# Four adaLN weight units of layer 0 move from the input projection to the output projection

## The reference, cut to what matters

```python
mod_lat = jnp.split(silu(c) @ ada_w[layer] + ada_b[layer], 6, axis=-1)
h = modulate(x, pre_mix_g, mod[0], mod[1])      # norm0: shift, scale
y = concat([a, b]) @ w_out                      # two attentions, one out projection
x = x + mod[2] * rms_norm(y, post_mix_g)        # norm1: gate
h = modulate(x, pre_ffn_g, mod[3], mod[4])      # norm1: shift, scale
x = x + mod[5] * rms_norm(conv_ffn(h), post_ffn_g)   # norm2: gate
```

## Time and profile before

| | kernel before |
|---|---|
| median of three timed executions | 1761.1 us (1760.04 to 1762.46) |
| profiled execution, span from first to last instruction | 1759.0 us |
| TensorE busy | 1687.6 us, 96% of the span |
| VectorE busy | 1026.4 us |
| ScalarE busy | 643.8 us |
| GpSimd busy | 277.3 us |
| mean granted TensorE clock | 0.991 |
| DMA | 224.27 MB, mean 127 GB/s |

### The profile page before, as it was taken

One profiled execution on the slowest core, in us unless ns is written; L12 is line 12 of the kernel. 1 busy time (PEld: TensorE's weight loads), 2 busy tenths in 40 slices (PEclk: granted clock), 3 DMA queues, 4 the chain that ended last, 5 costly groups with the idle time before them and its releaser, 6 DMA issues.

```text
span 1759.0 us, 26977 instructions
## 1 busy us (share of the span) xinstructions
PE 1687.6 (96%) x10042; PEld 1353.9 (77%) x10042; DVE 1026.4 (58%) x1938; ACT 643.8 (37%) x1090; POOL 277.3 (16%) x394
## 2 busy tenths in 40 slices
PE   5998899999999999999999999998999999999998
PEld 2876566668898888888888878875678788888886
DVE  4656565764747777777785681166743744443445
ACT  3323555663321212222324343245643333332343
POOL 1414333330300000000000031046421300000000
PEclk9999999999999999999999999999999999999999
DMA  8589441275513343434343543372503433332243
GB/s 314 191 262 304 108 111 24 46 95 190 190 52 97 103 136 106 132 113 127 97 144 108 179 168 126 114 186 58 145 10 108 144 96 95 95 95 81 86 133 132
DMA packets 265528, 224.27 MB, mean 127 GB/s; under 512 B 75224, under 2 KB 226136, under 8 KB 265432
## 3 DMA queue, kind: packets, MB, share of 16 engines
q1 hardware_dynamic: 257370, 206.42, 39.8%
q0 software_dynamic: 6048, 14.87, 2.2%
q10 hardware_dynamic: 2016, 1.71, 0.4%
HBM read 193.71 MB, written 29.25 MB: 127 GB/s over the span
## 4 chain that ended last, share of the span: by engine, by line
PE 84%; DVE 5%; ACT 3%; DMA 3%; issue 2%; POOL 2%; SPq 1%; ACTq 0%; DVEq 0%
PE ps L1252 30%; PE ps L852 11%; PE ps L853 11%; PE ps L854 11%; PE ps L1047 5%; PE ps L1129 4%; PE ps L1092 4%; PE ps L1262 2%; PE ps L1084 1%; PE ps L909 1%; ACT arena L1558 1%; PE ps L1237 1%; PE ps L1236 1%; PE ps L1238 1%; PE ps L1099 1%
## 5 line engine op out<-in xcount | busy, mean ns | idle before, releaser
L852 PE MATMUL ps<-w_hi,act_hi 128*128 128x512 f32 (+2 forms) x952 | 369.3, 388 | 2.1 <-DVE arena L2154 1.0
L853 PE MATMUL ps<-w_lo,act_hi 128*128 128x512 f32 (+2 forms) x952 | 364.7, 383 | 0.0
L854 PE MATMUL ps<-w_hi,act_lo 128*128 128x512 f32 (+2 forms) x952 | 364.7, 383 | 0.0
L1751 DVE TENSOR_TENSOR w_lo<-w_raw,w_hi 128x2048 fp32r<-128x2048 f32 (+4 forms) x114 | 206.9, 1815 | 243.8 <-ACT w_hi L1401 243.0
L1252 PE MATMUL ps<-act_lo,w_hi 128*128 128x512 f32 (+1 forms) x912 | 277.8, 359 | 0.0
L1252 PE MATMUL ps<-act_hi,w_hi 128*128 128x512 f32 (+1 forms) x912 | 276.2, 357 | 0.0
L1252 PE MATMUL ps<-act_hi,w_lo 128*128 128x512 f32 (+1 forms) x912 | 274.3, 355 | 0.0
L1401 ACT ACTIVATE w_hi<-w_raw 128x2048 fp32r<-128x2048 f32 (+3 forms) x108 | 168.7, 1562 | 270.9 <-PE ps L854 234.5
L852 PEld LDWEIGHTS ps<-w_hi,act_hi 128*128 128x128 f32 x952 | 179.7, 189 | 42.2 <-issue 8.8
L854 PEld LDWEIGHTS ps<-w_hi,act_lo 128*128 128x128 f32 x952 | 179.5, 189 | 34.0
L853 PEld LDWEIGHTS ps<-w_lo,act_hi 128*128 128x128 f32 x952 | 179.8, 189 | 32.5
(11 more groups left out here) (129 smaller groups left out, 2011.2 us busy)
## 6 DMA issues: line engine op xcount, KB each, us to landing
arena<-in_ada_w SPq DMA_DIRECT2D x44, 1024.0 KB, 8.5
w_raw<-in_ffn_up SPq DMA_DIRECT2D x88, 512.0 KB, 5.3
w_raw<-in_ffn_down SPq DMA_DIRECT2D x88, 256.0 KB, 3.0
w_raw<-in_odd_w_in SPq DMA_DIRECT2D x20, 512.0 KB, 4.6
arena<-mods SPq DMA_DIRECT2D x16, 512.0 KB, 6.5
proj_odd<-arena POOLq DMA_DIRECT2D x26, 256.0 KB, 2.4
x_after_mix<-arena SPq DMA_DIRECT2D x10, 512.0 KB, 2.9
arena<-x_after_mix SPq DMA_DIRECT2D x10, 512.0 KB, 5.2
```

The source lines that it names most:

```text
L852: mm(out_, s_hi, m_hi, start=start, stop=False)
L853: mm(out_, s_hi, m_lo, start=False, stop=False)
L854: return mm(out_, s_lo, m_hi, start=False, stop=stop)
L1751: V.tensor_sub(out_, full, hi.bitcast(fp32)).then_inc(sem_, 1)
```

## The change

Units 12 to 15 are no longer loaded and multiplied in in0. They get two buffers of their own, `out_raw`, in a part of the arena that the attention has freed by then, and two counts `late_in`. SP loads unit 12 when the last heads of SWA have been transposed, unit 13 when the attention's output is complete and ahead of the loads for norm1, and units 14 and 15 behind these loads, each when the unit two before it has left PSUM; the first feed-forward weights come behind them. PE multiplies them after tiles 2, 3, 4 and 5 of the second weight unit of out0. DVE takes them out of PSUM right behind `modulation`, and POOL stores them ahead of norm1.

```diff
+        out_raw = [arena[:, n * D:(n + 2) * D].rearrange("p (k c) -> p k c", k=KC) for n in (12, 14)]
+        late_in = [sem(f"late_in{i}") for i in range(2)]
-            ("in0", dict(t=22, th=NT, ...
+            ("in0", dict(t=12 + NT, th=NT, ...
-            ("out0", dict(mm=4 * N0, w=4, ev=2 * N0)),
+            ("out0", dict(t=4, mm=4 * N0, w=4, ev=2 * N0)),
-                  (4, 5): [8], (5, 2): [9], (5, 5): [10], (6, 2): [11], (6, 5): [12], (7, 5): [13], (6, 8): [14],
-                  (6, 11): [15]}
+                  (4, 5): [8], (5, 2): [9], (5, 5): [10], (6, 2): [11]}
+        ADA_IN_OUT = {2: 12, 3: 13, 4: 14, 5: 15}
...
SP
+            def out_unit(i):
+                g, slot = ADA_FIRST + i, i % 2
+                v = I["ada_w"][0].rearrange("(k p) c -> p k c", p=P)
+                sp.dma_start(out_raw[slot], v[:, :, g * ADA_COLS:(g + 1) * ADA_COLS]).then_inc(late_in[slot], 16)
+                b = I["ada_b"][0:1, g * ADA_COLS:(g + 1) * ADA_COLS]
+                sp.dma_start(late_bias[0:2, slot], b.to_broadcast([2, ADA_COLS])).then_inc(late_in[slot], 16)
-                last = {"norm1": 16, "norm2": 24, "norm3": 40, "norm4": 40}[name]
+                last = {"norm1": 12, "norm2": 24, "norm3": 40, "norm4": 40}[name]
-            for n, late in (..., (8, (12, 13)), (9, (14, 15))):
+            for n, late in (..., (8, ()), (9, ())):
...
+                if layer == 0:
+                    sp.wait_ge(left_free, base("swa", "tt") + SWA.prep_end(SWA.pairs - 1))
+                    sp.wait_ge(right_free, base("swa", "tt") + SWA.prep_end(SWA.pairs - 1))
+                    out_unit(12)
                 sp.wait_ge(o_lo, OL0 + base(nm, "hd"))
+                if layer == 0:
+                    out_unit(13)
                 mod_loads(nm)
                 gain_loads(nm)
                 x_moves(nm, range(2))
+                if layer == 0:
+                    for i in (14, 15):
+                        sp.wait_ge(t_free, ada_round(0, ADA_FIRST + i - 2) + 1)
+                        out_unit(i)
...
PE, ada_mm and out_projection
-                pe.wait_ge(early_in[i % 3], 32 * (i // 3 + 1))
+                if i < 12:
+                    raw = early_raw[i % 3]
+                    pe.wait_ge(early_in[i % 3], 32 * (i // 3 + 1))
+                else:
+                    raw = out_raw[i % 2]
+                    pe.wait_ge(late_in[i % 2], 32 * ((i - 12) // 2 + 1))
-                unit_mm((u + 1) % 2, tiles, 4, 512, (act_hi, act_lo), 4, False, True)
+                def after(b):
+                    if layer == 0 and b in ADA_IN_OUT:
+                        ada_mm(ADA_IN_OUT[b])
+                unit_mm((u + 1) % 2, tiles, 4, 512, (act_hi, act_lo), 4, False, True, after=after)
...
DVE, out_projection
                     if n == 0:
                         modulation(name)
+                        if layer == 0:
+                            for i in ADA_IN_OUT.values():
+                                early_evac(i)
...
POOL
             attention("swa", SWA)
+            for i in ADA_IN_OUT.values():
+                ada_store(0, ada_round(0, ADA_FIRST + i), i % 2, ADA_FIRST + i)
             norm("norm1")
```

More of the change, by code:

```diff
@@ L371, in build @@
             ("norm0", dict(norm_growth(NT, 0, 1, 2), mod=0)),
-            ("in0", dict(t=22, th=NT, mm=2 * accs[0] + 4 * NT, w=8, ev=accs[0] + 4 * NT,
+            ("in0", dict(t=12 + NT, th=NT, mm=2 * accs[0] + 4 * NT, w=8, ev=accs[0] + 4 * NT,
                          st=accs[0] - NT + 4 * NT, nsq=NT)),
             ("mla", att_growth(MLA)), ("swa", att_growth(SWA)),
-            ("out0", dict(mm=4 * N0, w=4, ev=2 * N0)),
+            ("out0", dict(t=4, mm=4 * N0, w=4, ev=2 * N0)),
             ("norm1", norm_growth(N0, 1, 1, 2)),
@@ L442, in build @@
         PV0 = OL0 = 1
-        ADA_IN0 = list(range(TURN0)) + list(range(TURN0 + NT, 22))
+        ADA_IN0 = list(range(TURN0)) + list(range(TURN0 + NT, 12 + NT))
         def ada_round(layer, g):
+            if layer == 0 and g - ADA_FIRST >= 12:
+                return base("out0", "t") + g - ADA_FIRST - 12
             if layer == 0:
@@ L741, in _ @@
             early_unit(2)
-            for n, late in ((4, (3, 4)), (5, (5, 6, 7)), (6, (8, 9)), (7, (10, 11)), (8, (12, 13)), (9, (14, 15))):
+            for n, late in ((4, (3, 4)), (5, (5, 6, 7)), (6, (8, 9)), (7, (10, 11)), (8, ()), (9, ())):
                 k_unit(n, *units[n])
@@ L863, in ada_mm @@
                 ring_free(r)
-                pe.wait_ge(early_in[i % 3], 32 * (i // 3 + 1))
+                if i < 12:
[4 more added lines that the diff above has]
+                    pe.wait_ge(late_in[i % 2], 32 * ((i - 12) // 2 + 1))
                 for k in range(KC):
                     c = k % GROUPS * GROUP
-                    last = mm(bank(6 + r % 2, ADA_COLS)[c:c + GROUP, :], silu[:, k, :], early_raw[i % 3][:, k, :],
+                    last = mm(bank(6 + r % 2, ADA_COLS)[c:c + GROUP, :], silu[:, k, :], raw[:, k, :],
                               start=k < GROUPS, stop=k >= KC - GROUPS)
@@ L1764, in early_evac @@
                     last = V.tensor_add(ada_row[:, i % 2, :], bank(6 + r % 2, ADA_COLS)[c:c + 2, :],
[L1765 removed]
+                                        ada_row[:, i % 2, :] if n else late_bias[0:2, i % 3 if i < 12 else i % 2, :])
                     if n < GROUPS - 1:
```

## The result

| | before | after |
|---|---|---|
| median of 11 timed executions each | 1761.74 us (1756.48 to 1764.08) | 1766.09 us (1764.11 to 1770.04) |
| ratio to before | 1 | 1.0035, 95% interval 1.0024 to 1.0046 |
| profiled execution, span | 1759.0 us | 1763.6 us |
| mean granted TensorE clock | 0.991 | 0.991 |

The changed kernel is slower by about 0.35%: 4.4 us by the medians, 4.6 by the two spans. The forecast was 1762.0 in 1756.5 to 1768, so the time lies inside the range. But it is above the forecast's own range (1758.5 to 1765.5), and by the forecast's measure of 0.2%, 3.5 us, it counts as slower. That had a chance of only 0.25; the likeliest case, no change, had 0.55.

The account below looks back on a forecast made before the run. PE, with 84% of the chain of work that ended last, was taken as the bound. 12.4 us back, 2 lost to head loads, 11.3 paid in out0 gave +0.9: 1762.0 us against 1761.1, range 1756.5 to 1768.

Parts of the forecast that it names:

- the likeliest case, no change: Whole kernel: the stall moves with the unit and changes place, not size; chance 0.55, own range 1758.5 to 1765.5 us.
- Both covers hold: Rival: heads in time, and mods not delayed by unit 13 or clock stays high; 3.9 us gained, 1757.2; chance 0.22.
- 12.4 back: In0: PE recovers 3.6 us from units 12, 13 and 15 and 8.8 us from unit 14's gap and slow restart.
- I take the early start ... and 7 us for the issues ...: 167.3, a loss of about 2 us.: Start of attention: first head loads land at 167.3, PE wants them at 165.5, losing about 2 us.
- my bounds (7.3): Start of attention: loss to the first head loads, from none at the early end to 7.3 us at the late end.
- Unit 13's load ... I take 3.0: Out0: unit 13's load ahead of the norm's loads delays DVE's modulation by 3.0 us, low end 0.
- PE stands still for 5.1 us, and I expect the clock to fall: Out0: PE waits 5.1 us for unit 14's load, landing taken as 5.6 us; clock falls to 1.2 GHz.
- Out0 becomes 11.3 us longer: Out0: its end moves from 424.2 to 435.5 us; low end 8.0 us longer, high end 17.8.
- the first heads are late: Rival, start of attention: head loads run as now, 7.3 us lost instead of 2, 1767.3; decides from 4.6; chance 0.10.
- Attention less than 7 us sooner: Refuting sign: the prediction is wrong if PE starts the attention less than 7 us sooner.
- the 166 to 168: Sign at the start of attention: transposes of the first head pair begin at 166 to 168 us.
- its bounds of 2 and 8: Sign in out0: one PE gap of about 5 us; the prediction is wrong if under 2 or over 8 us.

Follow-up runs that it names:

- small_stores: Changed kernel with the twelve c5 and c6 stores writing only the first eighth of their columns; total time says nothing, key loads' landing 3.6 us instead of 5.7.
- warm_gap: Changed kernel plus 30 filler transposes on PE in the wait for the first heads; 1765.58 us, ratio 1.0030 to the kernel before.
- mods_first: third_buffer with units 13 and 14 both loaded behind mods, gains and x; 1760.44 us, ratio 0.9996 to the kernel before.
- three_and_one: Units 12 to 14 stay in in0, only unit 15 goes to out0; 1761.25 us, ratio 1.0003 to the kernel before.
- two_and_two: Units 12 and 13 stay in in0, 14 and 15 go to out0, each with its own buffer; 1760.5 us, ratio 1.0006 to the kernel before.
- two_warm: two_and_two plus 22 filler transposes on PE in the wait before the first heads; 1758.84 us, ratio 0.9987 to the kernel before.
- third_buffer: Changed kernel with three buffers instead of two, unit 14 loaded behind x without waiting for unit 12; 1762.54 us, ratio 1.0022 to the kernel before.

## Why the prediction was right or wrong, point by point

The mechanism held in both places; one term of the sum was too small by five microseconds, and another a little too large. That the time is inside the range is owed to a range that was wide enough for the rivals. The prediction's sums come out to 0.1 us, save that *Both covers hold* takes 8.5 for out0, where the working has 8.0 as the low end and no row gives 8.5.

- *"12.4 back".* PE ends c6 12.9 us sooner. Some 0.5 of this was there ahead of the moved units (the last unit left in in0 starts 0.5 sooner). Right.
- *"I take the early start ... and 7 us for the issues ...: 167.3, a loss of about 2 us."* This is the step that failed, by its size. Its parts: SP began at 155.99 (155.5 forecast), the six issues took 5.85 (7), and the keys were issued at 162.51 as forecast (162.5), because two misses and 0.7 us behind the issues cancelled: luck. Their landing was taken from the earlier trace rows as 3.8 us; it was 5.7 in the median of the two, 6.5 on the chain. That row is of the second pair's keys; the first pair's, issued at 171.16 before, landed in 4.1 (the first fence below). The engines carried 286 GB/s meanwhile, and 350 after (the second fence, columns as in the earlier trace rows, one line before and one after): the stores of c5 and c6 came 12.9 us sooner as well, the keys only 8.7. Before, three stores of c5 ran beside the keys and those of c6 were issued from 175.13 on; after, the six of c6 were issued at 162.74 to 167.3, in the middle of it. I had let such stores weigh on the issues, not on the landing. small_stores shows it. The gap cost 4.4 us (12.9 - 8.4).

```profile
arena<-mla_kv SPq DMA_DIRECT2D x2, 192.0 KB, 4.1
```

```profile
171.20:175.30 4.10, 4.10 (x31) 2.81 (x30) 1.67 (x4) 2.21 (x4) 2.31 (x5) 1.00 1.15 286
162.50:168.30 5.80, 2.08 (x13) 1.56 (x11) 0.00 (x0) 3.02 (x6) 3.46 (x7) 0.88 1.15 350
```

- *A term left out.* I gave the wait in out0 its half clock, but not the wait that I forecast in front of the attention. Behind it 1.3 us went in the transposes and 1.2 more up to 189.5 (2.5 together, 8.44 to 5.94). Of these, 1.0 went in the twelve transposes at 180.52, where the clock is low again. warm_gap recovers the first 1.3 in the trace; that the timed execution is shorter by it is not shown. In all 7.1 us were lost up to the attention's end, near the end of my bounds (7.3), where I had taken 2; but those bounds were for the loads alone, which cost 4.4.
- *"Unit 13's load ... I take 3.0".* Modulation was 2.7 us later, and taking the load from in front of it brought modulation 2.1 us forward and gave 3.5 us of out0 back. Right.
- *"PE stands still for 5.1 us, and I expect the clock to fall".* 4.23 us, and 1.70 instead of 1.07 for the unit behind. Unit 14 was issued at 417.18 and taken up at 422.63, 5.4 us, where 5.6 was forecast. The fit of the Trainium skill, page "DMA: Bandwidth & Descriptors", section "Anatomy of one DMA — SWDGE (gpsimd) path", gives 4.4 for 1 MB, an estimate for the queue of gpsimd. This trace doesn't agree for SP's queue, though unit 15's load ran beside this one from 418.98 on.
- *"Out0 becomes 11.3 us longer".* 10.6. Four units without any wait cost 4.8 (mods_first), one 1.3 (three_and_one), two 2.5 (two_and_two): 1.2 to 1.3 each, forecast 1.2. Units 12, 13 and 15 waited for nothing, and the fourth split of DVE began 0.23 us after ACT's half, so evacuation didn't hold it up.
- *The sum.* 12.9 - 7.1 - 10.6 = -4.8 at norm1, where the forecast was 12.4 - 2 - 11.3 = -0.9. The rival "the first heads are late" (chance 0.10) comes nearest to what happened, but not by its mechanism alone: the late loads cost 4.4 us, just under the 4.6 from which it was to decide, and only with the half clock, which neither it nor the forecast had here, do they come to 7.1. Its argument against, "the 4 MB are gone", held for the issue of the keys, which came 8.7 us sooner. It overlooked that PE and the stores came sooner still. What sets the pace now are the c3 stores, six issues and the landing of the keys beside the c6 stores, one behind the other.
- *The signs.* Attention less than 7 us sooner was to refute it: it was 12.9 at the first transposes, 8.4 at the second, 7.2 at the first scores, and 5.75 at the attention's end. As a start of PE the sign was not met, but narrowly. The transposes of the first head pair began at 169.5, outside the 166 to 168 that I had given. The gap in out0, 4.23, was inside its bounds of 2 and 8.

Open is what makes two_warm faster than two_and_two (ratios 0.9987 and 1.0006, medians 1.7 us apart), if it is: in its profile the attention ends 2.1 us later (396.21 against 394.08).

## What to carry to other kernels

When work is taken out in front of a phase, all of that phase's producers come sooner, the stores that its first loads must share the engines with as well. A landing time read at one DMA load must not be used at another: take it from a stretch with similar GB/s, or keep the slow end. The two key loads of a pair landed in 3.8, 3.6, 4.1 and 5.7 us while the engines carried 207 (before, second pair), 243 (small_stores), 286 (before, first pair) and 350 GB/s (after); in the other runs without missing pieces or stores it was 5.2 to 6.7 us at 324 to 354 GB/s. And when a unit is moved behind another phase's loads, its buffer count and its place in the queue decide the price: here 10.6 us with two buffers ahead of the norm's loads, 4.8 with three behind them.

## What the runs showed that I had not expected

- Two units fewer in in0 bring the attention's end 4.7 us sooner, and four bring 4.3 to 5.75 in five profiles. The first two are all that can be told to be there, since the heads' loads take over. Three_and_one, with one unit fewer, brought nothing there (399.30 against 398.79).
- The issue of a small DMA can hold SP's queue for long. In third_buffer the bias of unit 14 (2 KB), issued behind unit 13's 1 MB, 5 MB of norm loads and 1 MB of its own weights, occupied it for 8.30 us:

```profile
401.43 8.30 SPq L603 DMA_DIRECT2D late_bias<-in_ada_b  x1
```
- Where the low clock falls behind the wait is not fixed. With filler (warm_gap) it left the first transposes and stayed in the later ones. It was on the first transposes in the changed kernel, on these and the first scores in mods_first, both without filler, and on the scores in two_warm with filler. That filler moves it is not shown.
